# The first norm of a hybrid SSD/gMLP/MoE step: weights applied in the copies out of PSUM, rows turned block by block

## The chip, the cores and the metric

The kernel runs on one core of a Trainium2 chip. The metric is device time in microseconds (us); the profile is of one execution of the program, and its times count from the start of its span.

## What is computed

One inference step of a one-layer decoder for 256 prompt rows and 64 sample rows (T = 320 rows, `D_MODEL` = 1024). The change lies in the first line of the layer, ahead of everything else:

```python
def rmsnorm(x, w):
    xf = x.astype(jnp.float32)
    y = xf * lax.rsqrt(jnp.mean(xf * xf, axis=-1, keepdims=True) + EPS)
    return (y * w.astype(jnp.float32)).astype(x.dtype)

hn = rmsnorm(x, norm_mix)
proj = hn @ w_in              # z, x/B/C, dt, u/v, gates
...                           # conv, SSD recurrence, chunked gMLP, gates
h = x + merged @ w_out
hf = rmsnorm(h, norm_ffn)
h = h + moe_ffn(hf, ...)      # top 4 of 32 experts
y = rmsnorm(h, norm_final)
```

## The kernel before, in words

All is f32. A product is computed in parts of type fp32r: the weight tile is split by ScalarE into a rounded high part and by VectorE into the rest (`split_tile`, L1510 and L1943), and the activations likewise into `hn_hi` and `hn_lo`. A 128-channel output tile is then 24 matmuls of 320 columns: 8 high times high (L833), 4 and 4 low weight times high rows (L835, L838), 8 high weight times `hn_lo` (L842). Tile number q writes `bank[q % 2]`: `dt` is tile 0, the first `v` tile is tile 1.

The 320 rows are three blocks, c = 0, 1, 2, of 128, 128 and 64 rows. The work before the first product:

- SyncE issues the loads on its queue: `x_prompt` (L524), `x_sample` (L525), then the chunks of `w_in` (L534): `dt` (128 KB), and `v` 0, 1 and 2 (1 MB each). They fill a ring of four; the fifth waits until the `dt` tile is computed.
- GpSimd zeroes a few columns of the ring, issues 12 loads on its own queue (L593 to L605: `norm_mix` broadcast to 128 partitions, 512 KB; seven small ones; `w_spatial`, `b_spatial`, and `v_norm_w` and `v_norm_b` broadcast, 512 KB each), and then builds the identity (L606, L607) and other constants up to `consts` (L645).
- ScalarE waits for both loads of `x`, squares and sums the three blocks (L1490) and takes the three square roots (L1499); VectorE turns the sums to variances in between (L1926). VectorE then takes the reciprocal (L1935) and computes `hn` = x times 1/std times `norm_mix` for each block in one `scalar_tensor_tensor` with two SBUF inputs (L1936).
- TensorE waits for all three blocks of `hn` and turns them, feature group k by feature group (k = 0 to 7, 128 features each), the three blocks of one k after each other into one PSUM bank of six (L814, called at its loop near L860). ScalarE copies the group out, rounded (`hn_hi`, L1516), and VectorE computes the rest (`hn_lo`, L1948), both while TensorE turns the next group. The first matmul of `dt` waits for all eight of `hn_hi`.

After that come, in an order written out by hand: `dt`, `v` 0, turns of small vectors (which wait for `consts`), `v` 1, turns of `w_spatial`, the other `v` tiles, and so on to the merge. SyncE issues no expert weight before the merge is done (`sp.wait_ge(S["merged"], 8)`, L546); from then on the experts' weights stream in through rings of slots, each load waiting for the slot's last use.

## Time and profile before

| what | us |
|---|---|
| median of 3 runs (lowest, highest) | 1549.33 (1548.80, 1550.73) |
| the profiled execution: its own time | 1552.08 |
| its span | 1550.3 |
| TensorE matmul busy | 1438.3 (93%) |
| VectorE busy, ScalarE busy | 603.4, 375.7 |
| DMA moved | 495.85 MB, mean 320 GB/s |

Busy times are sums over the whole span and say little of one stage: the mixer (to some 500 us) and the experts (after it) have different limits. The span is 1.8 us shorter than the execution's own time; what is taken off the span is taken off both.

### The profile page before, as it was taken

The numbers are of one execution on the slowest core, as the hardware profiler recorded it, in microseconds if no ns is written. First come the engines' busy times: TensorE is split into PE (matmuls) and PEld (weight loads), VectorE is DVE, ScalarE is ACT, GpSimd is POOL, SyncE is SP. The second block draws the span as 40 slices with busy tenths as digits, with TensorE's granted clock in tenths as the row PEclk, the third lists the DMA queues.
The fourth block names the chain that finished last, engine by engine and source line by source line (L and its number), as shares of the span: only waits on it lengthen the run. The fifth ranks groups of instructions, "written<-read, shape, count | busy, mean of one in ns | idle before, by whom it ended". The sixth has DMA issues, their size and how long they took to land.

```text
span 1550.3 us, 21980 instructions
## 1 busy us (share of the span) xinstructions
PE 1438.3 (93%) x8487; PEld 849.0 (55%) x8488; DVE 603.4 (39%) x1335; ACT 375.7 (24%) x626; POOL 200.3 (13%) x303
## 2 busy tenths in 40 slices
PE   5999999999999999989899998888999999989996
PEld 4989888898999544434434434432433434434432
DVE  4796888967543153212212212212122122122114
ACT  4556666656322241001001001000000000000002
POOL 4023434334920000000000000000000000000000
PEclk9999999999999999999999999998999999999998
DMA  7443555554454769999999999997999999999993
GB/s 223 154 126 113 144 166 144 157 154 146 145 162 141 280 252 428 427 429 427 428 430 427 428 430 427 429 428 298 407 428 429 428 430 427 428 430 428 427 430 156
DMA packets 123470, 495.85 MB, mean 320 GB/s; under 512 B 7204, under 2 KB 95324, under 8 KB 98008
## 3 DMA queue, kind: packets, MB, share of 16 engines
q1 hardware_dynamic: 85216, 471.74, 75.0%
q10 hardware_dynamic: 35888, 18.88, 4.1%
q0 software_dynamic: 2304, 4.40, 0.9%
q8 instruction: 40, 0.66, 0.2%
q14 instruction: 22, 0.18, 0.0%
HBM read 483.65 MB, written 11.34 MB: 319 GB/s over the span
## 4 chain that ended last, share of the span: by engine, by line
PE 63%; DMA 28%; DVE 5%; issue 2%; ACT 1%; SPq 1%; POOL 1%; DVEq 0%; ACTq 0%; POOLq 0%
DMA ring_b<-in_w_gu 27%; PE bank L1317 17%; PE bank L1370 9%; PE bank L1155 7%; PE bank L833 4%; PE bank L842 4%; PE bank L814 3%; PE bank L1270 3%; PE bank L838 2%; PE bank L835 2%; PE bank L1171 2%; PE bank L1080 2%; PE bank L1069 1%; PE bank L1426 1%; PE bank L1042 1%
## 5 line engine op out<-in xcount | busy, mean ns | idle before, releaser
L1317 PE MATMUL bank<-ring_b,xe 128*64 128x512 f32 x1280 | 352.4, 616 | 42.7 <-DMA ring_b<-in_w_gu 42.7
L1317 PEld LDWEIGHTS bank<-ring_b,xe 128*64 128x64 f32 x1280 | 116.4, 141 | 263.0 <-issue 262.6
L1317 PE MATMUL bank<-ring,xe 128*64 128x512 f32 x768 | 226.0, 594 | 5.5 <-DMA ring<-in_w_gu 5.1
L1370 PE MATMUL bank<-ring,actT 128*64 128x512 f32 x768 | 227.1, 596 | 0.0
L1490 ACT ACTIVATE swi<-swi 128x256 f32<-128x256 f32 x66 | 27.4, 417 | 568.3 <-DVE swi L2389 568.3
L2389 DVE TENSOR_SCALAR swi<-bank 128x256 f32<-128x256 f32 x64 | 27.2, 425 | 340.1 <-PE bank L1317 335.1
L1155 PE MATMUL bank<-rounded,ring_r 128*128 128x320 f32 x912 | 134.3, 308 | 1.7 <-DVE ring_r L2216 1.6
L1155 PEld LDWEIGHTS bank<-rounded,ring_r 128*128 128x128 f32 x912 | 133.2, 188 | 2.9 <-DVE ring_r L2216 2.8
L788 POOL TENSOR_TENSOR kept<-take 128x256 bf16<-128x256 bf16 x15 | 9.2, 613 | 875.8 <-PE bank L1352 875.8
L1317 PEld LDWEIGHTS bank<-ring,xe 128*64 128x64 f32 x768 | 75.0, 137 | 76.9 <-issue 76.9
L1370 PE MATMUL bank<-ring_b,actT 128*64 128x512 f32 x256 | 112.9, 594 | 4.3 <-ACT actT L1850 4.3
L1370 PEld LDWEIGHTS bank<-ring,actT 128*64 128x64 f32 x768 | 68.9, 137 | 63.1 <-issue 62.8
L2407 DVE TENSOR_TENSOR hid<-hid,bank 128x512 f32<-128x512 f32 (+1 forms) x90 | 57.8, 682 | 114.8 <-PE bank L1294 114.8
L833 PE MATMUL bank<-rounded,ring_r 128*128 128x320 f32 x456 | 82.7, 324 | 0.6 <-ACT rounded L1516 0.6
L842 PE MATMUL bank<-rounded,ring_r 128*128 128x320 f32 x456 | 76.6, 310 | 0.0
L1943 DVE TENSOR_TENSOR ring_r<-ring,ring_r 128x1024 fp32r<-128x1024 f32 (+1 forms) x61 | 74.0, 1226 | 3.3 <-ACT ring_r L1510 3.3
L833 PEld LDWEIGHTS bank<-rounded,ring_r 128*128 128x128 f32 x456 | 69.4, 193 | 2.0 <-issue 0.8
L842 PEld LDWEIGHTS bank<-rounded,ring_r 128*128 128x128 f32 x456 | 69.9, 189 | 0.0
L1370 PEld LDWEIGHTS bank<-ring_b,actT 128*64 128x64 f32 x256 | 33.8, 137 | 64.8 <-issue 64.6
L2500 DVE SCALAR_TENSOR_TENSOR ye_lo<-bank,routing,ye_hi 128x512 fp32r<-128x512 f32 x32 | 22.5, 746 | 113.2 <-ACT ye_hi L1861 113.2
L814 PE MATMUL bank<-ident,arena 128*128 128x128 f32 (+7 forms) x305 | 48.4, 283 | 18.1 <-DVE arena L1936 17.5
L1510 ACT CAST ring_r<-ring 128x1024 fp32r<-128x1024 f32 (+1 forms) x61 | 63.4, 1042 | 1.6 <-ACT arena L1490 1.0
(353 smaller groups left out, 2005.0 us busy)
## 6 DMA issues: line engine op xcount, KB each, us to landing
ring_b<-in_w_gu SPq DMA_DIRECT2D x83, 2048.0 KB, 17.1
ring<-in_w_down SPq DMA_DIRECT2D x50, 2048.0 KB, 18.8
ring<-in_w_gu SPq DMA_DIRECT2D x49, 2048.0 KB, 16.9
ring<-in_w_in SPq DMA_DIRECT2D x32, 1024.0 KB, 5.4
ring_b<-in_w_down SPq DMA_DIRECT2D x16, 2048.0 KB, 14.6
arena<-in_state_ssm ACTq DMA_DIRECT2D x16, 512.0 KB, 4.8
out<-arena ACTq DMA_DIRECT2D x16, 512.0 KB, 3.5
ring<-in_w_branch_ssd SPq DMA_DIRECT2D x8, 1024.0 KB, 5.5
```

The costliest lines, as they stand in the source:

```text
L814: return pe.transpose(out, in_, ident[0:in_.shape[0], 0:in_.shape[0]])
L833: pe.matmul(o, w_h[k], hn_hi[:, k, :], start=(k == 0), stop=False)
L835: pe.matmul(o, w_l[k], hn_hi[:, k, :], start=False, stop=False)
L838: pe.matmul(o, w_l[k], hn_hi[:, k, :], start=False, stop=False)
L842: mm = pe.matmul(o, w_h[k], hn_lo[:, k, :], start=False, stop=(k == KD - 1))
L1155: mm = pe.matmul(bank[4 * m + b][:, 0:T], w[:, k, m * P:m * P + P], v[:, k0 + k, :], start=(k == 0 and which != 4 and v is x_h and w is w_ ...
L1270: mm = pe.matmul(bank[6 + k // 4][:, (k % 4) * P:(k % 4) * P + P], part[0:rows(c), c, k * P:k * P + P], chosen_rows[0:rows(c), c, :], star ...
L1317: mm = pe.matmul(bank[q][side(h), :], xe[:, j, side(h)], moe_slot(2 * i + h)[:, 2 * FF * k + 512 * q:2 * FF * k + 512 * q + 512], start=Fa ...
L1370: mm = pe.matmul(bank[4 + half][side(h), :], actT[:, f, side(h)], w[:, D * k + 512 * half:D * k + 512 * half + 512], start=False, stop=(f ...
L1510: act.copy(hi, w).then_inc(S["split_hi"], 1)
L1943: dve.tensor_tensor(lo, w, hi.bitcast(F32), ALU.subtract).then_inc(S["split_lo"], 1)
L2407: dve.tensor_tensor(hid[0:rows(c), c, hb(c, half)], hid[0:rows(c), c, hb(c, half)], bank[6 + i % 2][0:rows(c), :], ALU.add).then_inc(S["cm ...
```

## The change

What the diff does:

- `norm_mix` is loaded once, as 8 rows of 128 (`nm_rows`), from ScalarE's queue; TensorE turns it to a column per feature group, and VectorE copies that to `nm_col`. The weights are applied per partition in the two copies out of PSUM: `act.mul` for `hn_hi`, `scalar_tensor_tensor` for `hn_lo`. `hn` itself is now x times 1/std, a `tensor_scalar` with one SBUF input.
- ScalarE starts with the prompt rows as soon as they are there, blocks 0 and 1 with their square roots, and then waits for the sample rows, which count on `rows_in` now. A square root of one element ahead of all of it loads the table.
- TensorE turns block by block (c outside, k inside), each block as soon as its `hn` is there. The eight groups need eight places: k = 0 to 5 have `bank[2 + k]`, k = 6 has `bank[1]`, and k = 7 lies in what is left of `bank[2]` and `bank[3]`, so its copies are two each. In block 2 the order is k = 7, 0, 1 to 6, and the copies of k start when its turn in block 2 is done.
- The first two tiles wait for `hn_hi` feature group by feature group.
- GpSimd builds the identity first, issues the small loads, makes four small copies, and then issues the four 512 KB loads. These count on `ws_in_s` (up to 64), so that `heads_in` ends at 32.

The hunks left out rename `rows_in` and renumber waits to match: `vec_ready` 1 to 2 and `vec_psum` 1 to 2 (the small vectors are the second on each now), `heads_in` 64 and `ws_in_s` 32 to `ws_in_s` 64.

```diff
@@ -188,6 +188,8 @@
         hn = place(base, 3, D)
         vtok = place(base + 4 * T, 3, D)
         nm_row = place(KD * T, D)
+        nm_rows = nm_row[0:KD, 0:P]
+        nm_col = nm_row[:, 512:512 + KD]
         vw_row = after(D)
 
         yT = place(base, PAIRS, T)
...
@@ -465,6 +467,18 @@
         def rows(c):
             return TILES[c][1]
 
+        def turned_rows(k, c):
+
+            if k < 7:
+                return bank[2 + k if k < 6 else 1][:, tok(c)]
+            return bank[3][:, T + 128 * (c - 1):T + 128 * (c - 1) + rows(c)] if c else bank[2][:, T:T + P]
+
+        def turned_parts(k):
+
+            if k < 7:
+                return [(slice(0, T), bank[2 + k if k < 6 else 1][:, 0:T])]
+            return [(slice(0, P), bank[2][:, T:T + P]), (slice(P, T), bank[3][:, T:512])]
+
         def tok(c):
             return slice(TILES[c][0], TILES[c][0] + TILES[c][1])
 
@@ -522,7 +536,7 @@
         @block.sync
         def _(sp):
             sp.dma_start(hid[:, 0:2, :], x_prompt[0].rearrange("(c p) d -> p c d", p=P)).then_inc(x_in, 16)
-            sp.dma_start(hid[0:NS, 2, :], x_sample.rearrange("b l d -> (b l) d")).then_inc(x_in, 16)
+            sp.dma_start(hid[0:NS, 2, :], x_sample.rearrange("b l d -> (b l) d")).then_inc(rows_in, 16)
             for n, c in enumerate(CHUNKS):
                 if n >= MIX_RING:
 
@@ -589,8 +603,11 @@
         @block.gpsimd
         def _(pool):
             link = chain(pool, pool_chain)
+            link(pool.memset(ident[:], 0.0))
+            link(pool.affine_select(out=ident[:], in_=ident[:], compare_op=ALU.not_equal, fill=1.0, base=0,
+                                    pattern=[[-1, P]], channel_multiplier=1))
             link(pool.memset(ring[:, 0, KD * H:DT_COLS], 0.0))
-            pool.dma_start(nm_row, norm_mix[0].partition_broadcast(P)).then_inc(rows_in, 16)
+            pool.sem_inc(S["ident_ready"], 1)
             pool.dma_start(small[0:H, 0:1], dt_bias[0].unsqueeze(1)).then_inc(heads_in, 16)
             pool.dma_start(small[0:H, 1:2], a_log[0].unsqueeze(1)).then_inc(heads_in, 16)
             pool.dma_start(junk[0:96, 0:P], conv_w[0].rearrange("k (t p) -> (k t) p", p=P)).then_inc(vecs_in, 16)
@@ -599,20 +616,16 @@
             pool.dma_start(junk[0:PAIRS, 2 * P:2 * P + 2], d_skip[0].rearrange("(j two) -> j two", two=2)
                            ).then_inc(vecs_in, 16)
             pool.dma_start(csin[0:KEEP * DB, :], state_conv[0].rearrange("b k c -> (b k) c")).then_inc(vecs_in, 16)
-            pool.dma_start(ws_in, w_spatial[0].rearrange("g t s -> t g s")).then_inc(ws_in_s, 16)
-            pool.dma_start(bs_row, b_spatial[0].partition_broadcast(P)).then_inc(ws_in_s, 16)
-            pool.dma_start(vw_row, v_norm_w[0].partition_broadcast(P)).then_inc(heads_in, 16)
-            pool.dma_start(vb_row, v_norm_b[0].partition_broadcast(P)).then_inc(heads_in, 16)
-            link(pool.memset(ident[:], 0.0))
-            link(pool.affine_select(out=ident[:], in_=ident[:], compare_op=ALU.not_equal, fill=1.0, base=0,
-                                    pattern=[[-1, P]], channel_multiplier=1))
-            pool.sem_inc(S["ident_ready"], 1)
             link(pool.tensor_copy(repeat[:].rearrange("p (b l) -> p b l", b=DB),
                                   ident[0:DS, 0:DS].unsqueeze(1).to_broadcast([DS, DB, DS])))
             link(pool.tensor_copy(ident_bf[:], ident[:]))
             for i in range(2):
                 s = slice(i * H, i * H + H)
                 link(pool.tensor_copy(pick_head[s, :], ident[s, s]))
+            pool.dma_start(ws_in, w_spatial[0].rearrange("g t s -> t g s")).then_inc(ws_in_s, 16)
+            pool.dma_start(bs_row, b_spatial[0].partition_broadcast(P)).then_inc(ws_in_s, 16)
+            pool.dma_start(vw_row, v_norm_w[0].partition_broadcast(P)).then_inc(ws_in_s, 16)
+            pool.dma_start(vb_row, v_norm_b[0].partition_broadcast(P)).then_inc(ws_in_s, 16)
             link(pool.memset(ones[:], 1.0))
             link(pool.affine_select(out=before[:], in_=ones[:], compare_op=ALU.is_ge, fill=0.0, base=-1,
                                     pattern=[[1, P]], channel_multiplier=-1))
...
@@ -827,9 +840,9 @@
                     pe.wait_ge(S["split_lo"], q + 1)
                     if q >= 2:
                         pe.wait_ge(S["proj_read"], q - 1)
-                    else:
-                        pe.wait_ge(S["hn_hi_ready"], KD)
                     for k in range(KD):
+                        if q < 2:
+                            pe.wait_ge(S["hn_hi_ready"], k + 1)
                         pe.matmul(o, w_h[k], hn_hi[:, k, :], start=(k == 0), stop=False)
                     for k in range(4):
                         pe.matmul(o, w_l[k], hn_hi[:, k, :], start=False, stop=False)
@@ -857,13 +870,14 @@
                 mm.then_inc(S["vt_psum"], 1)
 
             pe.wait_ge(S["ident_ready"], 1)
-            pe.wait_ge(S["hn_ready"], 3)
-            for k in range(KD):
-                if k >= 6:
-                    pe.wait_ge(S["hnT_ready"], k - 5)
-                for c in range(3):
-                    mm = turn(bank[2 + k % 6][:, tok(c)], hn[0:rows(c), c, k * P:k * P + P])
-                mm.then_inc(S["hnT_psum"], 1)
+            pe.wait_ge(rows_in, 32)
+            turn(bank[0][:, 0:KD], nm_rows).then_inc(S["vec_psum"], 1)
+            for c in range(3):
+                pe.wait_ge(S["hn_ready"], c + 1)
+                for k in (7, 0, 1, 2, 3, 4, 5, 6):
+                    mm = turn(turned_rows(k, c), hn[0:rows(c), c, k * P:k * P + P])
+                    if c == 2 and k < 7:
+                        mm.then_inc(S["hnT_psum"], 1)
 
             project("dt", 0)
             project("v", 0)
@@ -879,8 +893,8 @@
                 mm.then_inc(S["pre_psum"], 1)
             project("v", 1)
             turn_v(0)
-            pe.wait_ge(ws_in_s, 32)
-            pe.wait_ge(S["vec_ready"], 1)
+            pe.wait_ge(ws_in_s, 64)
+            pe.wait_ge(S["vec_ready"], 2)
             for g in range(GH):
                 mm = turn(bank[7 if g < 4 else 4][:, (g % 4) * P:(g % 4) * P + P], ws_in[:, g, :])
             mm.then_inc(S["ws_psum"], 1)
@@ -1489,14 +1503,30 @@
             def fn(out, in_, f, **kw):
                 return act.activation(out, in_, f, **kw)
 
-            act.wait_ge(x_in, 32)
-            for c in range(3):
+            act.dma_start(nm_rows, norm_mix[0].rearrange("(k p) -> k p", p=P)).then_inc(rows_in, 16)
+            act.wait_ge(S["ident_ready"], 1)
+            act.sqrt(small[0:1, 44:45], ident[0:1, 0:1])
+
+            def square(c):
+
                 fn(squared[0:rows(c)], hid[0:rows(c), c, :], ACT.Square,
                    accum_out=small[0:rows(c), 4 + c:5 + c]).then_inc(S["row_ss"], 1)
                 act.wait_ge(S["row_ss"], c + 1)
-            for c in range(3):
+
+            def root(c):
+
                 act.wait_ge(S["row_var"], c + 1)
                 act.sqrt(small[0:rows(c), 8 + c:9 + c], small[0:rows(c), 4 + c:5 + c]).then_inc(S["row_std"], 1)
+
+            act.wait_ge(x_in, 16)
+            square(0)
+            square(1)
+            root(0)
+            root(1)
+            act.wait_ge(rows_in, 32)
+            square(2)
+            root(2)
+
             def split_tile(q):
 
                 c, t = SPLIT[q]
@@ -1509,17 +1539,21 @@
                 w, hi, _ = tile_of(q)
                 act.copy(hi, w).then_inc(S["split_hi"], 1)
 
-            act.wait_ge(S["ident_ready"], 1)
             split_tile(0)
+            act.wait_ge(S["vec_ready"], 1)
             for k in range(KD):
-                act.wait_ge(S["hnT_psum"], k + 1)
-                act.copy(hn_hi[:, k, :], bank[2 + k % 6][:, 0:T]).then_inc(S["hn_hi_ready"], 1)
+                act.wait_ge(S["hnT_psum"], min(k, 6) + 1)
+                if k == 7:
+                    act.wait_ge(S["hnT_ready"], 2)
+                for at, b in turned_parts(k):
+                    mm = act.mul(hn_hi[:, k, at], b, nm_col[:, k:k + 1])
+                mm.then_inc(S["hn_hi_ready"], 1)
             for q in range(1, 3):
                 split_tile(q)
 
             q = tile_no("dt", 0)
             act.wait_ge(S["proj_ready"], q + 1)
-            act.wait_ge(heads_in, 64)
+            act.wait_ge(heads_in, 32)
             fn(dtmp[0:H, 0, :], bank[q % 2][0:H, 0:T], ACT.Identity, bias=small[0:H, 0:1]).then_inc(S["proj_read"], 1)
             split_tile(3)
             act.wait_ge(S["dt_abs"], 1)
...
@@ -1926,15 +1960,26 @@
                 return dve.tensor_scalar(dst, dst, 1.0 / count, EPS, ALU.mult, ALU.add)
 
 
-            for c in range(3):
+            def spread_first(c):
+
                 dve.wait_ge(S["row_ss"], c + 1)
                 var(small[0:rows(c), 4 + c:5 + c], c, D).then_inc(S["row_var"], 1)
-            dve.wait_ge(rows_in, 16)
-            for c in range(3):
+
+            def scale_first(c):
+
                 dve.wait_ge(S["row_std"], c + 1)
                 link(dve.reciprocal(small[0:rows(c), 12 + c:13 + c], small[0:rows(c), 8 + c:9 + c]))
-                dve.scalar_tensor_tensor(hn[0:rows(c), c, :], hid[0:rows(c), c, :], small[0:rows(c), 12 + c:13 + c],
-                                         nm_row[0:rows(c)], ALU.mult, ALU.mult).then_inc(S["hn_ready"], 1)
+                dve.tensor_scalar(hn[0:rows(c), c, :], hid[0:rows(c), c, :], small[0:rows(c), 12 + c:13 + c], None,
+                                  ALU.mult).then_inc(S["hn_ready"], 1)
+
+            spread_first(0)
+            spread_first(1)
+            scale_first(0)
+            scale_first(1)
+            spread_first(2)
+            dve.wait_ge(S["vec_psum"], 1)
+            dve.tensor_copy(nm_col, bank[0][:, 0:KD]).then_inc(S["vec_ready"], 1)
+            scale_first(2)
 
             def split_tile(q):
 
@@ -1945,8 +1990,10 @@
             split_tile(0)
             for k in range(KD):
                 dve.wait_ge(S["hn_hi_ready"], k + 1)
-                dve.tensor_tensor(hn_lo[:, k, :], bank[2 + k % 6][:, 0:T], hn_hi[:, k, :].bitcast(F32),
-                                  ALU.subtract).then_inc(S["hnT_ready"], 1)
+                for at, b in turned_parts(k):
+                    mm = dve.scalar_tensor_tensor(hn_lo[:, k, at], b, nm_col[:, k:k + 1], hn_hi[:, k, at].bitcast(F32),
+                                                  ALU.mult, ALU.subtract)
+                mm.then_inc(S["hnT_ready"], 1)
             for q in range(1, 3):
                 split_tile(q)
 
...
```

## Rows read from the trace of the kernel before

**Rows 1.** Windows: busy us (x instructions) of each engine, granted clock, DMA share, GB/s

```profile
40.00:60.00 20.00, 19.91 (x142) 19.55 (x141) 17.59 (x34) 11.37 (x15) 0.90 (x4) 1.00 0.56 171
200.00:300.00 100.00, 99.92 (x728) 88.90 (x728) 85.09 (x213) 68.43 (x125) 40.43 (x61) 1.00 0.53 156
620.00:700.00 80.00, 71.42 (x377) 29.19 (x378) 15.81 (x35) 4.44 (x9) 0.96 (x2) 1.00 1.01 428
```

**Rows 2.** The chain that ended last, 0 to 120: start us, us, what

```profile
1.32 6.65 DMA hid<-in_x_sample
...
17.53 7.39 PE bank L814 x24
24.94 0.43 ACT rounded L1516
25.51 2.47 PE bank L833 x8
27.98 1.07 PE bank L835 x4
...
30.11 1.63 PE bank L842 x8
...
48.79 1.17 PE bank L842 x8
```

**Rows 3.** Timeline, 10 to 17: start us, us, engine line operation, idle before

```profile
10.36 1.06 ACT L1490 ACTIVATE arena<-hid 64x1024 f32<-64x1024 f32 x1
...
11.52 1.28 ACT L1499 ACT_TABLE_LOAD   x1
12.82 0.39 ACT L1499 ACTIVATE small<-small 128x1 f32<-128x1 f32 x3
13.33 1.28 DVE L1936 SCALAR_TENSOR_TENSOR arena<-hid,small,arena 128x1024 f32<-128x1024 f32 x1
```

**Rows 4.** Timeline, ScalarE, last microseconds of the kernel

```profile
1539.65 0.20 ACT L1907 ACTIVATE small<-small 128x1 f32<-128x1 f32 x1 [1.78 <-DVE small L2543]
1539.76 0.61 ACT L1490 ACTIVATE swi<-hid 128x512 f32<-128x512 f32 x1
```

**Rows 5.** DMA issues, 0 to 60: queue, count, KB, median us to landing

```profile
hid<-in_x_prompt SPq DMA_DIRECT2D x1, 1024.0 KB, 5.5
...
arena<-in_v_norm_b POOLq DMA_DIRECT2D x1, 512.0 KB, 11.9
...
small<-in_dt_bias POOLq DMA_DIRECT2D x1, 0.1 KB, 7.0
```

**Rows 6.** DMA issues, 2.55 to 2.56: the first `v` chunk

```profile
ring<-in_w_in SPq DMA_DIRECT2D x1, 1024.0 KB, 17.3
```

**Rows 7.** DMA queues, 16 to 17: packets, MB, share

```profile
q1 hardware_dynamic: 90, 0.09, 25.9%
q0 software_dynamic: 84, 0.30, 75.3%
```

**Rows 8.** VectorE by shape, whole kernel: count, busy, mean ns

```profile
L2192 DVE SCALAR_TENSOR_TENSOR arena<-arena,bank 128x320 f32<-128x320 f32 x16 | 8.6, 537 | 2.4 <-PE bank L1042 2.4
...
L1956 DVE TENSOR_SCALAR arena<-arena 32x320 f32<-32x320 f32 x1 | 0.3, 308 | 0.0
```

**Rows 9.** Tile `arena`, 0 to 30: duration ns min/median/max

```profile
L633 POOL COPY arena<-samebatch x2: 179/690/1202, 13.5 to 14.7; 32x4 f32<-32x4 f32 x2
```

**Rows 10.** Timeline, TensorE, narrow windows at 18.9 and 19.2

```profile
18.69 0.42 PE L814 MATMUL bank<-ident,arena 128*128 128x128 f32 x1
19.04 0.37 PE L814 MATMUL bank<-ident,arena 64*128 64x64 f32 x1
```

**Rows 11.** ScalarE by line: a read of PSUM with a column operand

```profile
L1490 ACT ACTIVATE arena<-bank,small 32x320 f32<-32x320 f32 x1 | 0.5, 518 | 4.5 <-PE bank L842 4.5
```

**Rows 12.** Timeline, 19 to 35: `consts` done; the vector turns that wait for it

```profile
19.23 0.29 POOL L645 CAST row_expert<-slots_i 96x128 f32<-96x128 int32 x1
...
34.95 0.14 PEld L814 LDWEIGHTS bank<-ident,arena 120*128 120x128 f32 x1
```

More of the change, by code:

```diff
@@ L336, in build @@
         x_in = sem("x_in")
-        rows_in = sem("rows_in")
+        rows_in = sem("sample_and_norm_in")
         vecs_in = sem("vecs_in")
@@ L645, in _ @@
             pool.tensor_copy(row_expert[:], slots_i[0:96, 0:P]).then_inc(consts, 1)
-            pool.wait_ge(S["vec_ready"], 1)
+            pool.wait_ge(S["vec_ready"], 2)
             pool.wait_ge(S["pre_ready"], 2)
@@ L1568, in read_conv @@
                 else:
-                    act.wait_ge(S["vec_ready"], 1)
+                    act.wait_ge(S["vec_ready"], 2)
                 act.copy(raw[:, n % 2, KEEP:SPAN], b[:, 0:SEQ])
@@ L1972, in read_v @@
                 dve.tensor_copy(vtok[0:NS, 2, m * P:m * P + P], b[0:NS, 2 * P:3 * P]).then_inc(S["vt_ready"], 1)
-            dve.wait_ge(S["vec_psum"], 1)
+            dve.wait_ge(S["vec_psum"], 2)
             dve.tensor_copy(convv[:], bank[4][:, 0:120])
@@ L2055, in _ @@
                 split_tile(tile_no("z", i) + 4)
-            dve.wait_ge(heads_in, 64)
+            dve.wait_ge(ws_in_s, 64)
             for c in range(3):
@@ L2114, in add_mix_bias @@
                                   ).then_inc(S["mix_read"], 1)
-            dve.wait_ge(ws_in_s, 32)
+            dve.wait_ge(ws_in_s, 64)
             add_mix_bias(0)
```

## The prediction

> **What bounds the kernel now.** I read the windows first, to learn which resource is full in which stage. The reader is to see two things in [rows 1]. From 40 us into the mixer TensorE is busy 19.91 of 20 us, and 99.92 of 100 later, at half of the DMA share: the mixer goes at TensorE's pace. In the experts (620 to 700) the DMA share is 1.01 at 428 GB/s and TensorE has gaps: they go at the pace of the loads. Both stages only start when what is before them is done: the products of the mixer follow each other in one written order, and no expert weight is issued before the merge. So time that is saved ahead of the first full product moves everything behind it, if nothing in the first 40 us has another cause. I then read the chain of waits from its start [rows 2]: nothing but one serial line. The sample rows land at 1.32 + 6.65 = 8.0. Then three squares, a table load of 1.28 and the roots [rows 3], three scalings, and only then, at 17.53, the 24 turns in 7.39. The last copy starts at 24.94, the first `dt` matmul at 25.51. That is 25 us in which TensorE does no product, and the change works on nearly all of them. Two paces in [rows 2] matter below: 4 matmuls of 320 columns in 1.07 (0.267 each, one column per cycle at 1.2 GHz) in `dt`, and 8 in 1.17 (0.146) later, the level of 2.4 GHz. The 8 in 1.63 at 30.11 are a mix: with n at the low level 0.267 n + 0.146 (8 - n) = 1.63, n = 3.8, so the level rose near 31.1, 5.6 us after the first `dt` matmul. The rows at 40 to 60 grant 1.00.
>
> **Step 1, the start of the squares.** `x_prompt` is issued half a microsecond ahead of `x_sample`, at 0.8, and took 5.5 [rows 5]: it is there at 6.3. ScalarE no longer waits for 8.0. Two squares took 10.36 - 8.0 = 2.4 [rows 2, 3], so both prompt blocks are summed at 8.7. The load of the root's table (1.28) goes to the idle time before 6.3. Whether a square then asks for another table is shown at the end of the kernel: there a square starts 0.11 after a root, and no load lies between them [rows 4]. If it did ask, each change back would cost 1.28; I take none. From root to scaling it is 13.33 - 12.82 = 0.51 [rows 3], so the first scaling starts at 9.2.
>
> **Step 2, the scaling.** The three-operand form of 1024 columns took 1.28 [rows 3]. The new form has one SBUF input; a `TENSOR_SCALAR` of 320 columns took 308 ns [rows 8]. Scaled with the columns that is 0.99 for 1024. A line through two three-operand forms, 537 ns at 320 columns [rows 8] and 1280 at 1024, leaves 0.20 fixed; with that the new form is 0.20 + 3.2 x 0.108 = 0.55. I take 0.75, between the two, bounds 0.55 and 1.28. The first `hn` is ready at 9.95, against 17.53 for the first turn before: 7.6 earlier. Block 1 follows at 10.9, block 2 (square at about 9.1, since the sample rows land no later than 8.0; variance, the copy of the column, root, scaling) at about 12.4. It is not needed before 14.4, so up to 2 us of extra there cost nothing.
>
> **Step 3, the norm weights.** Eight rows of 512 B replace 512 KB of broadcast. The new wait stands in front of every turn on TensorE, so all of it is queued behind this small load and behind the sample rows (8.0). The nearest row is a small load on GpSimd's queue, 7.0 from issue to landing [rows 5]: issued near 0.8, that is 7.8. Below 9.95 it costs nothing. The upper bound is in the rivals. The one turn and the column's copy lie beside the scalings, below 0.3 us each.
>
> **Step 4, the turns.** The 24 took 7.39, 0.308 on average [rows 2]. From a 128-row turn to a 64-row one it is 19.04 - 18.69 = 0.35 [rows 10], so the other two steps of a group share 0.57. In the new order 16 turns of 128 rows stand together: 16 x 0.28 = 4.5, then 8 of 64 rows at 0.30 = 2.4. They end at 9.95 + 6.9 = 16.85, bounds 16.2 and, at the old mean, 17.35. Nothing lies between them: places for all eight groups are free.
>
> **Step 5, the copies and the first eight matmuls.** Copies can't start before block 2's turns, at 14.45 + 0.6 = 15.05. Before, a copy (0.43) lay hidden in each group's 0.92 of turns and only the last one showed. Now the copies are closer together than they can run: a read of PSUM with a column operand took 518 ns on ScalarE [rows 11]; with 0.07 overlapped I take a step of 0.45, seven of them and 0.65 for the two-part copy of k = 7: `hn_hi` is complete at 18.85. TensorE follows group by group, eight at 0.267 from 16.85, so 19.0, and not before 18.85 + 0.27 = 19.1. With 0.2 for eight waits inside the row of matmuls: 19.3. Before it was 27.98 [rows 2]. **This is the gain: 8.7 us.** VectorE's part has two-operand reads of 537 ns [rows 8], so it is complete at about 15.6 + 7 x 0.5 + 0.75 = 19.9; it is needed by `dt`'s last eight at 19.3 + 8 x 0.267 = 21.4. Hidden by 1.5 us.
>
> **Step 6, the rest of `dt` and the clock.** If the level rises as long after the first product as before, at 16.85 + 5.6 = 22.4, the 16 left take 3.75 (11.6 at the low level, 4.4 at the high), as before (27.98 to 31.74). I take 0, bounds: 1.0 gained or lost, since 8 matmuls sooner or later at the other level are worth 8 x 0.12.
>
> **Step 7, the first `v` tile's weights.** This is what is late next. The chunk is issued near 2.55 and took 17.3 [rows 6]: it lands at 19.8, before as now unless the queues change. It shares the 16 engines with GpSimd's large loads, which had 75% of them to its 26% at 16 to 17 [rows 7]; the last issued took 11.9 [rows 5]. Now 512 KB are gone and the other four start, I estimate, 1.3 us later (the identity and four small copies ahead of them, one issue less). That leaves SP's queue alone for longer, and I expect 13 to 18. Even 19.8 costs nothing: ScalarE's split (about 1.0) and VectorE's (1.2) end at 22.1, and `v` 0 starts at 19.3 + 3.75 = 23.05. Other moved waits: the vector turns need `consts`, done at 19.5 before and not later than 20 now, and come at 34.95 - 8.7 = 26.2 [rows 12]. The turns of `w_spatial` wait for all four large loads now, done by about 21; they come 5 us after the vector turns. Both hidden.
>
> A small price may be on GpSimd's side. In [rows 9] a copy of 4 columns took 179 ns once and 1202 ns when it started 0.1 us after a 1.28 us scaling with two SBUF inputs: it waited for it. In the new kernel it can also be the scaling that waits, behind one GpSimd instruction at 9.2, up to 0.3 us; kept for the range. The Trainium skill speaks against the change here: "SBUF — State Buffer", "Who interferes with whom", says that VectorE's two-port modes, which a `tensor_scalar` can enter and a scaling with two tensor inputs cannot, hold the port pair that GpSimd uses for the whole instruction, whichever came first. By that rule the faster scaling is bought with the lock, and the sum would be at most 0.3 worse on the path; by the row alone, none. The row agrees with the lock itself.
>
> **Sum.** 8.7 gained on the first eight products, 0 behind. The profiled execution took 1552.1 with a span of 1550.3; the same execution with the change would take 1543.4. The median is 2.7 lower than the profiled one, 1549.3, so I forecast **1540.6**.
>
> **Rivals.**
>
> *The level rises sooner.* TensorE's turns will stand close together and run straight into products, without the pause from 24.9 to 25.5. If the activity of the turns counts, the level is 2.4 GHz from about the first product: 12 or more products at 0.12 less, 1.6 us: 1539.0. For it: TensorE is never idle from 9.95 on. Against: 7.39 us of turns at the low level did not raise it before [rows 2]. [...] 15%.
>
> *The first `v` chunk is late.* It decides from a landing of 20.7 on (23.05 less the 2.3 of splits). If SP's queue gets the engines later, say a landing at 25, 4.3 us of the gain go: 1544.9. For: queues share the engines, 26% for this one. Against: less is ahead of it than before. 8%.
>
> *The column lands late, and the kernel is slower.* All turns wait behind it. It eats the gain from a landing at 9.95 + 8.7 = 18.7. The long landing of [rows 6], 17.3, would give 18.1, still 0.6 better than before; a landing at 20 gives 1550.6. Against: eight packets, issued before anything large is on the engines, and small loads needed 7.0. 3%.
>
> *The gain is given back.* The diff does what it says, but something later than 40 us has its own time, and the result is 1549. For it only that the first 100 us have VectorE at 17.59 of 20 as well [rows 1]; against, that its work too hangs on the products. 3%.
>
> **Chances.** Forecast 71%, sooner level 15%, late chunk 8%, slower 3%, given back 3%. Smallest difference that can be told here: about 0.2%, 3 us. All but the last two are more than that: faster 94%, same 3%, slower 3%. Range: down to the sooner level with turns at their lower bound and a little luck of the experts' stage, 1537.8; up with the scaling at its upper bound (0.5), turns at the old mean (0.5), the level 1.0 later, the lock 0.3, and half of the late chunk: 1545.0.
>
> **What would show it.** In the profile after: the first square near 6.3 and no table load behind it; scalings of 0.55 to 0.9; first turn near 10, 24 turns in under 7.4; ScalarE's copies in steps of 0.45 and the eighth product done near 19.3; the first `v` product near 23, ended by VectorE's split and not by a DMA; the windows from 40 us on like those of before. Wrong would be: the turns waiting for anything but `hn`; scalings at 1.28; a TensorE gap ahead of `v` 0; or a first product 8.7 sooner with a span that is not.

## The result, and the profile after

The changed kernel takes 1540.81 us (median of 5 runs, 1539.01 to 1542.95), the kernel before 1550.73 beside it (5 runs, 1548.80 to 1552.35): 0.9937 of the time, interval 0.9923 to 0.9950. The forecast was 1540.6. That the two agree to 0.2 us is luck: the gain was 9.9 instead of 8.7, and the kernel before took 1.4 more here than the 1549.33 that the forecast was taken from. Timed a second time (e12 below) the changed kernel took 1543.12 against 1550.28, 0.9952, interval 0.9936 to 0.9969. The profiled execution took 1540.44, its span is 1538.7.

The windows after, with the columns of [rows 1]: both long stages have the same limits as before, TensorE in the mixer and the DMA engines in the experts.

```profile
40.00:60.00 20.00, 20.00 (x146) 19.74 (x145) 12.63 (x25) 9.54 (x12) 0.00 (x0) 1.00 0.44 136
200.00:300.00 100.00, 99.94 (x731) 88.40 (x731) 89.51 (x224) 68.26 (x123) 38.43 (x58) 1.00 0.51 148
620.00:700.00 80.00, 73.19 (x433) 31.77 (x430) 18.97 (x47) 6.10 (x13) 0.96 (x2) 0.98 1.01 428
```

The chain of waits from its start, in the form of [rows 2]:

```profile
0.80 5.23 DMA hid<-in_x_prompt
6.05 1.16 ACT arena L1504 x2
...
8.85 0.80 DVE arena L1972
9.69 4.72 PE bank L827 x24
14.54 3.62 PE bank L846 x8
18.16 1.07 PE bank L848 x4
19.23 1.07 PE bank L851 x4
20.29 1.88 PE bank L855 x8
```

The serial line is gone from 8.0 us on: the first turn (a transpose on TensorE) starts at 9.69 (17.53 before [rows 2]), the turns take 4.72 for 7.39, and the copies no longer stand in the chain by themselves, since the first eight products lie beside them. The timeline of the same stretch shows what each engine does:

```profile
1.46 1.28 ACT L1508 ACT_TABLE_LOAD   x1 [1.46 <-PEq L2629]
...
7.54 0.24 PE L827 MATMUL bank<-ident,arena 8*128 8x8 f32 x1 [7.54 <-DMA hid<-in_x_sample]
...
8.41 0.39 ACT L1519 ACTIVATE small<-small 128x1 f32<-128x1 f32 x2
8.85 0.78 DVE L1972 TENSOR_SCALAR arena<-hid,small 128x1024 f32<-128x1024 f32 x1
9.69 3.28 PEld L827 LDWEIGHTS bank<-ident,arena 128*128 128x128 f32 x16 [2.00 <-DVE arena L1972]
...
11.06 0.74 DVE L1972 TENSOR_SCALAR arena<-hid,small 64x1024 f32<-64x1024 f32 x1
11.28 0.83 POOL L632 MEMSET causal<- 128x320 f32 x1
...
13.29 0.93 PEld L827 LDWEIGHTS bank<-ident,arena 64*128 64x128 f32 x8 [0.33 <-issue]
13.87 3.60 ACT L1549 ACTIVATE rounded<-bank,arena 128x320 fp32r<-128x320 f32 x9 [2.66 <-PE bank L827]
14.43 3.89 DVE L1994 SCALAR_TENSOR_TENSOR rounded<-bank,arena,rounded 128x320 fp32r<-128x320 f32 x9 [2.19 <-ACT rounded L1549]
14.54 3.62 PE L846 MATMUL bank<-rounded,ring_r 128*128 128x320 f32 x8
...
20.09 2.07 PE L855 MATMUL bank<-rounded,ring_r 128*128 128x320 f32 x8
22.00 1.33 PE L846 MATMUL bank<-rounded,ring_r 128*128 128x320 f32 x8
```

The reader is to see three limits after each other: the squares and VectorE's scaling up to 9.69, TensorE's turns up to 13.87, ScalarE's copies up to 17.5 (nine in 3.60, and eight products spread over the same 3.62). The last line is the first product of `v`: 22.00, against 31.57 before. This is the mark by which I compare the kernels below; a second one is a set of 13 turns in the middle of `v`, at 51.79 after and 61.36 before. Both are 9.57 earlier.

The chunk of `v` 0, 17.3 from issue to landing before [rows 6], takes 10.6 now and lands at 13.2:

```profile
ring<-in_w_in SPq DMA_DIRECT2D x1, 1024.0 KB, 10.6
```

**How well the total can be told.** The spans differ by 11.6, the marks by 9.57. The rest is in the experts, whose first and last weight loads of TensorE are in these two lines, of before and of after (count, ns, first to last start):

```profile
L1317 PEld LDWEIGHTS bank<-ring_b,xe x1280: 132/137/232, 559.6 to 1512.9; 128*64 128x64 f32 x183
```

```profile
L1331 PEld LDWEIGHTS bank<-ring_b,xe x1280: 132/137/232, 549.8 to 1500.8; 128*64 128x64 f32 x183
```

953.3 us and 951.0. The change touches nothing there, and the fourteen profiled executions of this document gave 950.4 to 955.3 for this stretch; the same changed kernel, profiled again (e12 below), 953.2. So 9.6 us are the change's, and 2 are what one execution differs from another by.

The mixer behind the second mark scatters too. From the mark to the first of these loads it is 498.2 us before and 498.0 after, but 495.0 to 499.4 over the fourteen. This window of the changed kernel shows why; the granted clock is third from the end:

```profile
103.60:107.00 3.40, 3.40 (x15) 3.26 (x14) 2.18 (x10) 2.07 (x3) 0.00 (x0) 0.50 0.00 0
```

In this stretch e2 and e5 have no such fall to 0.50 (495.0, 495.1), e1, e7, e11 and e12 have one of 3.4 us (496.1 to 496.8), six executions have 6.8 us of it (497.8 to 498.2; before and changed are among them), and e9 and e4 have 10.2 us (499.2, 499.4). So 3.4 us at 0.50 cost some 1.5 us. That the two profiles compared here have equally many is luck; it is why they can be compared to the tenth, and a single time can't.

### The profile page after: what moved, and what is told of

Same layout as the page of the kernel before. It is cut to its first block, busy times and chain, and to the rows that moved or that the text cites. A ratio compares the mean times of both kernels' runs of the same rounds, so it can differ in the third digit from the quotient of the medians.

```text
span 1538.7 us, 21986 instructions
## 1 busy us (share of the span) xinstructions
PE 1434.9 (93%) x8488; PEld 848.8 (55%) x8489; DVE 601.3 (39%) x1337; ACT 374.7 (24%) x627; POOL 198.3 (13%) x302
## 4 chain that ended last, share of the span: by engine, by line
PE 63%; DMA 28%; DVE 5%; issue 2%; ACT 1%; SPq 1%; POOL 1%; DVEq 0%; ACTq 0%; POOLq 0%
DMA ring_b<-in_w_gu 27%; PE bank L1331 17%; PE bank L1384 9%; PE bank L1169 7%; PE bank L846 4%; PE bank L855 4%; PE bank L1284 3%; PE bank L827 3%; PE bank L851 2%; PE bank L848 2%; PE bank L1185 2%; PE bank L1094 2%; PE bank L1083 1%; PE bank L1440 1%; PE bank L1056 1%
## 5 line engine op out<-in xcount | busy, mean ns | idle before, releaser
L2547 DVE SCALAR_TENSOR_TENSOR ye_lo<-bank,routing,ye_hi 128x512 fp32r<-128x512 f32 x32 | 22.6, 747 | 113.2 <-ACT ye_hi L1895 113.2
L2263 DVE TENSOR_TENSOR ring_r<-ring,ring_r 128x2048 fp32r<-128x2048 f32 x18 | 43.3, 2403 | 49.4 <-ACT ring_r L1752 49.3
```

The costliest lines, as they stand in the source:

```text
L2263: dve.tensor_tensor(lo, v, hi.bitcast(F32), ALU.subtract).then_inc(S["split_lo"], 1)
```

## The experiments

Each is the changed kernel with one edit, except e11 and e9 (several) and e12 (none). First the marks, in us from the span's start. The column x is the landing of `x_prompt`, which moved by some tenths by itself. The last column says when TensorE's clock went from 1.2 to 2.4 GHz, down again and up again: the first rise is where the steps of its instructions halve, what follows is the granted clock.

| kernel | x | first turn | first `dt` product | first `v` product | 13 turns | clock up, down, up |
|---|---|---|---|---|---|---|
| before | 6.3 | 17.53 | 25.51 | 31.57 | 61.36 | 31.0 |
| changed | 6.0 | 9.69 | 14.54 | 22.00 | 51.79 | 21.7 |
| e12, changed again | 6.3 | 9.94 | 14.79 | 22.35 | 52.14 | 22.2 |
| e1, no feed by group | 6.3 | 9.90 | 17.83 | 23.24 | 53.04 | 21.8 |
| e2, turns after all rows | 6.1 | 11.94 | 16.79 | 23.72 | 53.51 | 16.0, 19.4, 22.8 |
| e3, turns in the old order | 6.4 | 12.20 | 19.52 | 25.01 | 54.82 | 23.7 |
| e4, squares together | 6.2 | 12.54 | 17.39 | 25.08 | 54.93 | 25.4 |
| e5, table not loaded ahead | 6.4 | 12.60 | 17.37 | 24.23 | 54.03 | 16.4, 19.8, 23.2 |
| e6, broadcast load added back | 6.0 | 9.71 | 14.56 | 22.02 | 51.82 | 21.7 |
| e8, three-operand scaling | 6.2 | 10.36 | 15.21 | 22.33 | 52.13 | 15.0, 18.4, 21.8 |
| e10, row loads later still | 6.2 | 9.78 | 14.11 | 20.73 | 50.54 | 12.6, 16.0, 19.4 |
| e7, idle TensorE kept busy | 6.2 | 9.86 | 13.14 | 19.88 | 50.59 | 5.1, 15.3, 18.7 |
| e11, e7 and e10 | 6.4 | 10.05 | 13.34 | 18.93 | 48.75 | 6.8 |
| e9, e11 and no pauses | 6.4 | 10.04 | 13.34 | 19.27 | 49.08 | 5.7 |

Times of those that were timed: e3 1545.57 (7 runs, 0.9959 of before, 0.9945 to 0.9973), e4 1545.27 (5, 0.9968, 0.9953 to 0.9984), e7 1539.93 (6, 0.9934, 0.9920 to 0.9947), e9 1537.23 (5, 0.9917, 0.9902 to 0.9933), e12 1543.12 (6, 0.9952, 0.9936 to 0.9969). The others ran once: e1 1540.61, e2 1544.68, e5 1541.95, e6 1543.58, e8 1543.64, e10 1541.59, e11 1538.06. One run is uncertain by about 3, so for these only the marks count.

**e1: no feed by feature group.**

```diff
-                    for k in range(KD):
-                        if q < 2:
-                            pe.wait_ge(S["hn_hi_ready"], k + 1)
+                    if q < 2:
+                        pe.wait_ge(S["hn_hi_ready"], KD)
+                    for k in range(KD):
```

> The changed kernel, but the first two tiles wait for all eight feature groups of hn_hi before their first product. Theory (products and copies overlap, and that overlap is worth what it hides): in the changed kernel the first product starts at 14.54 and the eighth is done at 18.16, with the last copy near 17.5. Here the first can start at 17.5 and eight at 0.267 end at 19.7: 1.5 us later, and the first v product starts near 23.5 instead of 22.0. Rival (the clock decides): the level of TensorE's clock rises a fixed time after the first product, so products that start 3 us later also end 3 x 0.45 more later, and the first v product is at 24 to 25; or the level comes at the same time anyway and the loss is below 1 us.

Measured: the eight products start at 17.83 and take 2.47, so they are done at 20.30, 2.1 later than in the changed kernel (0.2 of it is the later `x_prompt`); the theory had 1.5. The first `v` product is only 1.24 later: the clock level rose at 21.8 against 21.7, so nearly half of the loss came back. The rival's second branch holds in its reason: products that start 3 us later do not bring the level 3 us later.

**e2: the turns wait for all three blocks.**

```diff
-                pe.wait_ge(S["hn_ready"], c + 1)
+                pe.wait_ge(S["hn_ready"], 3)
```

> The changed kernel, but TensorE waits for all three blocks of hn before the first turn; the order of the turns stays block by block. Theory (the early start of blocks 0 and 1 is worth the time by which block 2's turns come sooner): the third hn is ready at 11.8, 24 turns in 4.7 end at 16.5 instead of 14.4, the first copy starts near 15.8 instead of 13.9, the first v product near 23.9 instead of 22.0: 1.9 us later. Rival (ScalarE's copies are the limit and wait for something else too): below 0.5 us later.

Measured: the first `v` product 1.72 later, the first turn and the first `dt` product 2.25 later. The clock level was up during part of the turns and came back at 22.8 here, which it did not in the changed kernel, so the start of the `dt` products is the cleaner mark: the early start of blocks 0 and 1 is worth some 2.2.

**e3: the old order of turns.**

```diff
-            for c in range(3):
-                pe.wait_ge(S["hn_ready"], c + 1)
-                for k in (7, 0, 1, 2, 3, 4, 5, 6):
-                    mm = turn(turned_rows(k, c), ...)
-                    if c == 2 and k < 7:
-                        mm.then_inc(S["hnT_psum"], 1)
+            pe.wait_ge(S["hn_ready"], 3)
+            for k in range(KD):
+                if k == 7:
+                    pe.wait_ge(S["hnT_ready"], 2)
+                for c in range(3):
+                    mm = turn(turned_rows(k, c), ...)
+                mm.then_inc(S["hnT_psum"], 1)
```

(ScalarE waits for `hnT_psum` k + 1 again.)

> The changed kernel with the old order of turns (feature group outside, the three blocks inside, after all three hn); the eight places, the weights in the copies and the feed by feature group stay. It tells where 2.2 us came from that I had not forecast: 24 turns took 4.72 in the new order against 7.39 before. Theory A (alternating 128-row and 64-row turns costs the time): a group takes 0.92 as before, the turns run from 11.8 to 19.2, the copies are hidden again, the eighth product is done near 21.3 instead of 18.16, and the first v product starts near 25.1. Theory B (the turns were slow before for another reason, the copies reading beside them or the clock): 24 turns take about 4.7, end at 16.6, the eighth product is done near 18.7 and v starts near 22.6. Time over the kernel before: A 7 us less, B 9 us less.

The timeline of TensorE in e3:

```profile
12.20 7.39 PE L827 MATMUL bank<-ident,arena 128*128 128x128 f32 x24 [4.14 <-DVE arena L1973]
19.52 2.50 PE L846 MATMUL bank<-rounded,ring_r 128*128 128x320 f32 x8
```

Theory A, to the hundredth: 7.39 as before. The same 24 turns cost 4.72 when the sixteen of 128 rows stand together and the eight of 64 rows after them, and 7.39 when each third one has 64 rows. Single turns in narrow windows give the paces. In the changed kernel they start at 12.52, 12.73, 12.94 (128 rows), 13.30 (the first of 64 rows) and then every 0.11: steps of 0.21 and 0.11, and one of 0.35 at the change. In e3 a group starts at 12.20, 12.47, 12.82, and the next at 13.12. A group would be 0.53 by the first paces and is 0.92, so 0.38 per group goes with the mixing, and seven groups more of it are the 2.67 that separate the two. Most of it is in one place; the loads of the turns' stationary rows, in the kernel before, stand still ahead of each one of 64 rows:

```profile
18.12 0.58 PEld L814 LDWEIGHTS bank<-ident,arena 64*128 64x128 f32 x3 [0.33 <-issue]
19.04 0.59 PEld L814 LDWEIGHTS bank<-ident,arena 64*128 64x128 f32 x3 [0.33 <-issue]
```

The changed kernel has this 0.33 once, in its line at 13.29 above. What the engine does in it is not shown. Against e2, which also waits for all rows, e3 is 1.3 later at the first `v` product, 0.26 of it from its first turn, and e2 had its level up for a part of the way: the order's part is about 1.

**e4: squares and roots as before.** ScalarE waits for `x_in` and `rows_in`, takes three squares, then three roots; VectorE's order follows.

> The changed kernel, but ScalarE waits for prompt and sample rows, does three squares and then three roots, as the kernel before; the table load stays ahead of them. Theory (start is worth its serial length): the sample rows are there at 7.5, three squares take 3.5, a root and a reciprocal 0.5, a scaling 0.8, so the first turn is near 12.4 instead of 9.7 and everything behind it 2.7 us later, the first v product near 24.7. Time about 7 us below the kernel before instead of 9.9. Rival (the gain is in the order of turns and the feed, the early rows are hidden by block 2): the copies wait for block 2 anyway, whose hn is at 14.2 here instead of 11.8, so the loss is at most 1 us.

Measured: the sample rows landed at 7.7, first turn and first `dt` product 2.85 later, first `v` product 3.08 later. The rival is out: a start that is 2.85 later is passed on whole.

**e5: no table load ahead.**

```diff
-            act.sqrt(small[0:1, 44:45], ident[0:1, 0:1])
```

> The changed kernel without the square root of one element that loads the table ahead of the data. Theory: a load of 1.28 us comes back between the second square and the first root, the first turn is at 11.0 instead of 9.7 and the first v product near 23.3 instead of 22.0; no other load, since a square works in the root's table. Rival (the rows wait for more than this): the first v product less than 0.5 us later.

Both missed it. ScalarE in e5:

```profile
6.42 1.28 ACT L1504 ACT_TABLE_LOAD   x1 [6.42 <-DMA hid<-in_x_prompt]
7.72 1.06 ACT L1504 ACTIVATE arena<-hid 128x1024 f32<-128x1024 f32 x1
...
10.07 1.28 ACT L1518 ACT_TABLE_LOAD   x1
11.36 0.30 ACT L1518 ACTIVATE small<-small 128x1 f32<-128x1 f32 x2
11.56 1.04 ACT L1504 ACTIVATE arena<-hid 64x1024 f32<-64x1024 f32 x1
```

Two loads, not one: with nothing loaded, the first square asks for a table of its own, and here its load comes behind the wait for the data. In the kernel before, whose ScalarE program begins with the wait for the data and that square, it lay ahead of the data:

```profile
0.80 1.28 ACT L1490 ACT_TABLE_LOAD   x1 [0.80 <-PEq L2582]
```

Why it lies behind the wait in e5, where a DMA issue and the wait for the identity come first, is not shown. The first turn is 2.9 later, of which 0.3 is the later `x_prompt`; the two loads are 2.56. The line at 11.56 also confirms [rows 4]: a square behind a root loads nothing. The first `v` product is only 2.2 later; the level of the clock came in another way here (see e10).

**e6: the broadcast load added back.**

```diff
+            pool.dma_start(vw_row, norm_mix[0].partition_broadcast(P)).then_inc(broadcast_in, 16)
             pool.dma_start(small[0:H, 0:1], dt_bias[0].unsqueeze(1)).then_inc(heads_in, 16)
...
+            pool.wait_ge(broadcast_in, 16)
             pool.dma_start(vw_row, v_norm_w[0].partition_broadcast(P)).then_inc(ws_in_s, 16)
```

> The changed kernel with the 512 KB broadcast load of the norm weights added back as GpSimd's first load, into a region that v_norm_w overwrites later (GpSimd waits for it before it issues that one); nothing reads it. Theory (the load is off the critical path, it only takes engines from the queue of w_in): the sample rows land near 8.0 instead of 7.5, the first v chunk lands near 16 to 18 instead of 13.2, and the first v product still starts at 22.0 within 0.3. Rival (the load was part of what the start waited for): x_prompt lands later than 6.05, and all behind it moves by as much; or the chunk lands after 20 and the first v product with it.

Measured: marks at 22.02 and 51.82, no change. The first chunk took 11.9 from issue instead of 10.6, the next 19.1 instead of 17.6, so it landed at 22.6, where ScalarE took it up at 22.65. The sample rows came no later (7.4). The load is worth nothing by itself, with 0.1 us to spare. It also explains only 1.3 of the 6.7 us by which the first chunk's way became shorter (17.3 to 10.6); the rest came, most likely, with the later issue of the four large loads, which no run undoes by itself.

**e8: the scaling with two SBUF inputs.**

```diff
-                dve.tensor_scalar(hn[...], hid[...], small[0:rows(c), 12 + c:13 + c], None, ALU.mult)
+                dve.scalar_tensor_tensor(hn[...], hid[...], small[0:rows(c), 12 + c:13 + c],
+                                         small[0:rows(c), 48:49].to_broadcast([rows(c), D]), ALU.mult, ALU.mult)
```

(Column 48 is set to 1.0 by VectorE ahead of it.)

> The changed kernel with the scaling of hn in the three-operand form again (times 1/std, times a one that is read with step 0), two SBUF inputs. Theory: each scaling takes 1.28 instead of 0.76, the first turn comes 0.5 later, the third hn at 13.3 to 13.5 is still just in time for block 2's turns, and the first v product starts 0.5 later, near 22.5. Rival (block 2 decides): 1.5 us later.

Measured: the first scaling takes 1.28, first turn and first `dt` product 0.67 later (0.17 of it `x_prompt`), first `v` product 0.33, with the level up for a part of the way. Block 2 does not decide.

**e7: TensorE kept busy while it waits.**

```diff
             pe.wait_ge(S["ident_ready"], 1)
+            for _ in range(22):
+                pe.matmul(bank[7][:, 0:P], ident[:, :], ident[:, :], start=True, stop=True)
             pe.wait_ge(rows_in, 32)
```

> The changed kernel with 22 products of the identity with itself (128 columns, f32, into bank 7, read by nobody) on TensorE as soon as the identity is there, while TensorE is idle until 9.7. Theory (TensorE's clock level rises on activity of any kind of product, and dt pays for its low level): the turns and the dt products run at 2.4 GHz. Copies then start at about 12.3 (third hn at 11.8) instead of 13.9 and end near 15.9, the other 16 products take 2.3 instead of 4.0, and the first v product starts near 18.3 to 18.6 instead of 22.0: 3.5 us less in the total, about 1537. Rival (identity products do not raise it, or the level falls again before dt): the first v product at 22.0, no gain, or up to 0.5 us lost if the 22 end after 9.7. Second rival (the chunk of v 1, which lands near 21, is late then): part of the gain is given back before 30.

Measured: 2.12 sooner at the first `v` product, 1.20 at the 13 turns. The identity products do raise the level: 14 records in 3.1 us up to 5.00, 19 in 1.9 us from 5.10 on (a product is two records), and the 24 turns took some 2.9 in all.

```profile
1.87:5.00 3.13, 3.13 (x14) 3.13 (x15) 0.00 (x0) 1.08 (x2) 2.52 (x5) 1.00 0.97 293
5.10:7.00 1.90, 1.90 (x19) 1.90 (x19) 0.00 (x0) 0.76 (x1) 1.77 (x6) 1.00 1.17 269
```

But it fell again. The windows of e7, columns as in [rows 1], granted clock third from the end:

```profile
5.00:15.00 10.00, 8.24 (x62) 6.74 (x60) 5.48 (x16) 6.85 (x17) 8.68 (x24) 1.00 1.10 297
15.30:18.60 3.30, 3.30 (x11) 2.79 (x12) 3.18 (x7) 2.65 (x5) 2.58 (x9) 0.50 1.04 413
18.70:22.00 3.30, 3.30 (x24) 3.30 (x24) 1.50 (x3) 1.13 (x2) 0.00 (x0) 1.00 1.06 378
```

Ahead of the stretch at 0.50 (1.2 GHz) TensorE had fed products with pauses. And the second rival holds too: the next chunk was late.

```profile
21.39 1.05 ACT L1542 CAST ring_r<-ring 128x1024 fp32r<-128x1024 f32 x1 [0.79 <-DMA ring<-in_w_in]
```

**e10: the four large loads further back**, ahead of the `iota` for `slots`.

> The changed kernel with only the four 512 KB loads moved further back, behind most of GpSimd's constants. Theory (the large row loads are off the critical path in the changed kernel, later is worth nothing): the v 1 chunk lands before 17 instead of at 21, the first v product is at 22.0 and the 13 turns at 51.8 within 0.3. Rival (late loads are waited for): the turns of w_spatial, at 30.9 in the changed kernel, come later and the 13 turns with them.

The next chunk landed 13.2 after issue instead of 17.6, as expected. The marks were 1.26 sooner, which neither side expected, and it isn't the loads: no wait for them is on the chain in the changed kernel. The turns took 3.94 instead of 4.72, and the windows show why:

```profile
13.00:16.20 3.20, 2.78 (x15) 1.59 (x14) 2.20 (x5) 2.76 (x7) 2.78 (x8) 0.96 1.10 340
16.30:19.60 3.30, 3.30 (x12) 2.89 (x13) 3.17 (x7) 2.63 (x5) 2.69 (x7) 0.53 1.09 370
19.70:22.00 2.30, 2.30 (x18) 2.30 (x17) 1.29 (x3) 1.07 (x2) 0.00 (x0) 1.00 1.02 414
```

The level rose during the turns, fell in the fed products and rose again at 19.4, where the changed kernel reaches it at 21.7. The same is in e2, e5 and e8, which did not move the loads; it is absent in e1, e3, e4, e6 and e12. So it comes and goes between executions. From the first turn to the first `v` product it is 12.3 to 12.5 in the changed kernel, e12, e4 and e6, and 11.8, 11.6, 12.0 and 10.95 in e2, e5, e8 and e10: one mark is uncertain by up to 1.4 us.

**e11: e7 and e10 together.**

> e7_warm with the four 512 KB loads moved behind GpSimd's constants, without the products between the fed ones. Theory: the first v product is near 19.9 as in e7_warm, and the 13 turns come at 49.7, since the v 1 chunk is there: the 0.9 us that e7_warm lost between the first v product (2.1 sooner) and the 13 turns (1.2 sooner) come back. Rival (they were lost to VectorE's or ScalarE's work on dt): the 13 turns at 50.6 as in e7_warm.

13 turns at 48.75, 3.04 sooner than in the changed kernel, more than the theory's 2.1. From the first `v` product to the 13 turns it is 29.82, as in the changed kernel (29.79) and not 30.71 as in e7: the chunk was e7's loss. The rest is that the level did not fall in this execution, with the pauses as in e7.

**e9: e11 and no pauses**, by products that nobody reads, into unused columns of `dt`'s bank.

```diff
                         pe.matmul(o, w_h[k], hn_hi[:, k, :], start=(k == 0), stop=False)
+                        for _ in range(3 if q == 0 and k < 7 else 0):
+                            pe.matmul(bank[0][:, T:512], w_h[k], hn_hi[:, k, 0:512 - T], start=False, stop=False)
...
+            pe.matmul(bank[0][:, T:T + P], ident[:, :], ident[:, :], start=True, stop=True)
             project("dt", 0)
```

> The changed kernel with three things: the 22 identity products while TensorE is idle (as in e7_warm); products between the eight fed ones that nobody reads (three of 192 columns after each of the first seven, and one of the identity behind the turns), so that TensorE has no pauses while ScalarE's copies pace it; and the four 512 KB loads moved behind GpSimd's constants. Theory (in e7_warm the level fell at 15.25 because of the pauses between fed products, and the v 1 chunk at 21.4 held ScalarE's split): now the level stays at 2.4 GHz from 5 us on, the first product is at 13.1, the eighth done near 16.8, the first v product near 19.1 instead of 22.0, the v 1 chunk lands before 17, and the 13 turns that are at 51.79 in the changed kernel come at 48.9: 2.9 us less, about 1538. Rival (the fall at 15.25 has another cause, or the extra products delay the fed ones): the level falls as before and the first v product is at 19.9 or later. Rival 2 (another engine's work is the limit behind v 0): the first v product is 2.9 sooner and the 13 turns less than 2 sooner.

Measured: first `v` product 19.27, 13 turns 49.08 (48.9 expected), 1537.23. Beside it on one chip:

**e12: the changed kernel again.**

> The changed kernel itself once more, beside e9_warm_kept on the same chip. First v product at 22.0 and 13 turns at 51.8 within 0.3, time near 1541; what its trace differs in from the first one is what one execution is uncertain by.

1543.12, and marks 0.35 later, with `x_prompt` 0.3 later and the level 0.5 later. e9's interval over the kernel before (0.9902 to 0.9933) lies below e12's (0.9936 to 0.9969): e9 is better than both kernels beside it, by 13 us and by some 6. It overlaps with that of the changed kernel's first series (0.9923 to 0.9950). Its marks give 2.7 to 3.1 of that 6; the rest is not explained. The changed kernel's own two medians are 2.3 apart, and the means of these two series, 1537.9 and 1542.4, only 4.5. What the added products among the fed ones do for it is not shown, since e11 kept the level without them.

## Why the prediction was right

The mechanism was the one forecast: one serial line, nothing with a time of its own behind it, and the gain passed on to the end. e3 and e4 show this in the total too: 3.0 and 3.1 us lost at the first `v` product are 2.4 and 2.2 more in the median than e12's, or 4.8 and 4.5 more than the first series'. One term of the sum lay outside its bounds (step 4). Step by step:

- Step 1: squares from 6.05 (6.3 forecast), no second table load, first scaling at 8.85 (9.2). Right; e4 puts a price of 3.1 on it. The table's load ahead is a condition of it that I had put at 1.28 and that is 2.56 in e5.
- Step 2: 0.78 for 0.75. Right. Of the lock with GpSimd, the changed kernel shows one side: the `causal` memset that started 0.22 after a scaling took 0.83, and 0.36 before the change. No scaling took longer than 0.78, so on VectorE's side it cost nothing here. The Trainium skill ("SBUF — State Buffer", "Who interferes with whom") has both sides; the trace agrees with it where GpSimd is the one that comes second. I had called [rows 9] the same lock; by that section it is another case, a VectorE instruction with two SBUF inputs, which contends with a GpSimd instruction that reads SBUF and not with one that only writes it. The trace of the kernel before agrees: beside the scaling of 14.72 to 16.00 a memset of 320 columns took 0.35 and was not held up.

```profile
14.96 0.35 POOL L634 MEMSET running<- 32x320 f32 x1
```

- Step 3: the column's turn was at 7.54, released by the sample rows. Hidden, as forecast.
- **Step 4 was mis-sized**: 24 turns at 6.9 (bounds 6.25 to 7.4), measured 4.72, outside the bounds. I took 0.28 for a 128-row turn and 0.30 for a 64-row one from a mixed series, where the price of mixing is inside the numbers. Unmixed they are 0.21 and 0.11. [Rows 10] had the hint, a step of 0.35 ahead of the 64-row turn, and I spread it evenly.
- Step 5: copies from 13.87 (15.05), eighth product done at 18.16 (19.3): 1.1 sooner, 0.26 from the start and 0.9 from step 4. The copies took 3.60 for 3.8, and the eighth product ended 0.69 behind them for 0.45 (the 0.2 for the waits in it had no row). Since the copies are the limit behind the turns, only the turns ahead of the first copy counted: of the 2.2 us by which step 4 was off, 0.9 came through. That an error of 2.2 in a term moved the total by only 1 is the order's merit, not the forecast's.
- Step 6: 18.16 to 22.00, 3.84, where the kernel before took 31.57 - 27.98 = 3.59. The level rose 7.2 us after the first product, not 5.6: 0.25 lost, within the 1.0 allowed.
- Step 7: the chunk was at 13.2 (13 to 18), and e6 shows the broadcast load's absence to be worth nothing at 22.

So 8.7 + 1.1 (step 5) - 0.25 (step 6) = 9.6, the shift of both marks; the medians are 9.9 apart in the first series and 7.2 in the second, and 9.6 lies inside both intervals.

The rival of a sooner level was in part right. In the profiled execution it did not happen, but in e2, e5, e8 and e10 the level rose during the block-by-block turns, which it had not done in 7.39 us of alternating ones, neither before nor in e3. The Trainium skill ("TensorE: Matmul & The Clock Gate", "Part 4: PE-mode transpose") says that the full clock does not engage for transposes; these four executions disagree, since TensorE had done nothing but turns in them before the rise, and by them my 15% was too low: four of nine executions with block-by-block turns. Whether alternating turns can't raise it is not shown by two executions. What I had not seen is that the level falls again in the fed products, so it was worth 0.3 to 1.4 where it came, not 1.6. The late chunk, the late column and the lost gain did not come; the chunk of `v` 1 came due in e7, where TensorE was 2 us sooner.

## What to carry to other kernels

Write the start of a kernel as a chain of waits and ask of each engine which piece it could begin with; here the early blocks, the feed by feature group, the order of the turns and a table load were each worth 1 to 3 us when undone one at a time. Take a duration for a new order only from rows in that order: a mean over mixed shapes holds the cost of mixing. And when an engine is pulled forward, look at the second transfer in the queue, not the first.

## What the runs showed of the hardware

- Turns of 128 and of 64 rows: 24 in 4.72 us when grouped by kind, 7.39 when every third has 64 rows (changed kernel, e3), some 0.38 more per group of three, at 1.2 GHz.
- Turns alone raised TensorE's level in e2, e5, e8 and e10, and f32 products of an identity in e7, e9 and e11 (in e7 it then stayed from 5 to 15 us, with nothing but these and turns up to 12.7). Where it was up, fed products with pauses between them were followed by 0.50 in e2, e5, e7, e8 and e10 and not in e11; without pauses (e9) it stayed.
- Later in the mixer the granted clock was at 0.50 for 0 to 10.2 us in all, differently in two executions of one kernel (6.8 in the changed kernel, 3.4 in e12), and each 3.4 us of it cost some 1.5 us (495.0 to 499.4 us from the 13 turns to the first expert load).
- The granted clock that the windows print for the first microseconds is 1.00 in the changed kernel too, where products of 320 columns in steps of 0.267 show 1.2 GHz up to 21.7. Before the first recorded change the column says nothing, and the pace of the products decides.
